# A decoder trunk on one core: x by features, packed weights, and a new order for the first weight slots

## The reference

```python
def rmsnorm(x, g):
    xf = x.astype(jnp.float32)
    y = xf * lax.rsqrt(jnp.mean(xf * xf, axis=-1, keepdims=True) + EPS)
    return (y * g.astype(jnp.float32)).astype(x.dtype)

def short_conv_mixer(h, w_in, w_conv, w_out):
    bg, cg, xv = jnp.split(h @ w_in, 3, axis=-1)
    return (bg * causal_dwconv(cg * xv, w_conv)) @ w_out

def reference(x, norm_mix, ...):
    for i in range(DEPTH):
        h = rmsnorm(x, norm_mix[i])
        if i < N_A_LAYERS:
            x = x + short_conv_mixer(h, a_w_in[i], a_conv[i], a_w_out[i])
        ...
        x = x + conv_ffn(rmsnorm(x, norm_ffn[i]), ...)
```

## Time and profile before

| | us |
|---|---|
| median of 3 runs (lowest to highest) | 579.64 (579.08 to 579.85) |
| the profiled execution, and its span | 579.68, 577.9 |
| PE busy | 570.1 (99%) |
| DVE busy | 422.0 (73%) |
| ACT busy | 318.4 (55%) |
| POOL busy | 22.5 (4%) |

### The profile page before, as it was taken

The page is one execution under the profiler, slowest core; times in us unless marked ns, Lnnn a source line. Parts: engine busy times, 40 slices in busy tenths (PEclk is TensorE's granted clock), DMA queues, the critical chain, the costliest instruction groups (busy, mean ns, idle before and its releaser), DMA issues.

```text
span 577.9 us, 8023 instructions
## 1 busy us (share of the span) xinstructions
PE 570.1 (99%) x3064; PEld 493.6 (85%) x3064; DVE 422.0 (73%) x514; ACT 318.4 (55%) x389; POOL 22.5 (4%) x26
## 2 busy tenths in 40 slices
PE   8999999999999999999999999999999999999996
PEld 7888988888888888888888899888888888888885
DVE  6898886678666666776887688896786666667764
ACT  5734463566645455456555666745656454554543
POOL 1233000000000000000000000000000000000000
PEclk9999999999999999999999999999999999999999
DMA  8996558445665565555655444285455665664001
GB/s 270 349 349 228 196 183 289 177 151 163 204 218 205 167 212 195 173 177 183 219 154 177 180 146 146 82 282 180 149 168 197 219 208 162 212 196 170 0 1 73
DMA packets 80866, 107.03 MB, mean 185 GB/s; under 512 B 1888, under 2 KB 71872, under 8 KB 80832
## 3 DMA queue, kind: packets, MB, share of 16 engines
q1 hardware_dynamic: 80240, 104.78, 55.0%
q10 hardware_dynamic: 592, 1.77, 0.9%
HBM read 105.50 MB, written 1.05 MB: 184 GB/s over the span
## 4 chain that ended last, share of the span: by engine, by line
PE 91%; DVE 2%; ACT 2%; issue 1%; SPq 1%; DMA 1%; POOL 0%; POOLq 0%; ACTq 0%
PE pair L1202 37%; PE pair L1210 19%; PE acc L1271 7%; PE acc L1275 7%; PE acc L1273 7%; PE pair L1258 5%; PE pair L1263 3%; PE acc L1178 1%; PE acc L1179 1%; PE acc L1177 1%; DVE wgt L761 1%; DMA raw<-in_a_w_in 1%; PE pair L1285 1%; ACT wgt L434 1%; ACT acc L454 0%
## 5 line engine op out<-in xcount | busy, mean ns | idle before, releaser
L761 DVE TENSOR_TENSOR wgt<-raw,wgt 128x2048 fp32r<-128x2048 f32 x92 | 211.4, 2302 | 53.6 <-ACT wgt L434 53.3
L1202 PE MATMUL pair<-hA,wgt 128*128 128x512 f32 x864 | 205.4, 391 | 0.2 <-DVE wgt L761 0.2
L434 ACT ACTIVATE wgt<-raw 128x2048 fp32r<-128x2048 f32 x93 | 177.5, 1911 | 22.9 <-PE acc L1275 21.5
L1202 PEld LDWEIGHTS pair<-hA,wgt 128*128 128x128 f32 x864 | 160.1, 188 | 32.3 <-issue 0.4
L1210 PEld LDWEIGHTS pair<-hA,wgt 128*128 128x128 f32 x864 | 107.8, 192 | 2.4
L1210 PE MATMUL pair<-hA,wgt 128*128 128x256 f32 x864 | 108.5, 283 | 0.0
L1271 PE MATMUL acc<-wgt,kq_hi 128*128 128x512 f32 x156 | 48.0, 389 | 0.0
L1275 PE MATMUL acc<-wgt,kq_lo 128*128 128x512 f32 x156 | 48.0, 389 | 0.0
L1273 PE MATMUL acc<-wgt,kq_hi 128*128 128x512 f32 x156 | 48.0, 389 | 0.0
L529 ACT ACTIVATE scratch<-scratch 128x512 f32<-128x512 f32 x22 | 13.9, 632 | 59.7 <-DVE scratch L878 59.7
L543 ACT ACTIVATE scratch<-pair 128x512 f32<-128x512 f32 x20 | 11.9, 595 | 58.3 <-PE pair L1210 58.3
(11 more groups left out here) (180 smaller groups left out, 601.9 us busy)
## 6 DMA issues: line engine op xcount, KB each, us to landing
raw<-in_ffn_w_up SPq DMA_DIRECT2D x44, 1024.0 KB, 5.1
raw<-in_ffn_w_down SPq DMA_DIRECT2D x22, 1024.0 KB, 4.9
raw<-in_a_w_in SPq DMA_DIRECT2D x10, 1024.0 KB, 11.8
raw<-in_w_kv SPq DMA_DIRECT2D x8, 1024.0 KB, 5.3
raw<-in_a_w_out SPq DMA_DIRECT2D x4, 1024.0 KB, 5.5
raw<-in_b_w_q SPq DMA_DIRECT2D x4, 1024.0 KB, 5.2
raw<-in_b_w_o SPq DMA_DIRECT2D x4, 1024.0 KB, 5.0
xs<-in_x SPq DMA_DIRECT2D x4, 256.0 KB, 4.2
```

What stands on the lines that cost most here:

```text
L434: act.activation(split_slot(s)[0], raw[:, s % RAW, :], ACT.Copy).then_inc(w_hi_ready, 2 if s + 1 in AHEAD else 1)
L761: dve.tensor_tensor(wlo, raw[:, s % RAW, :], whi.bitcast(F32), ALU.subtract).then_inc(w_lo_ready, 2 if s + 1 in AHEAD else 1)
L1202: last = pe.matmul(pair[b][:, e, :].rearrange("p (a n) -> p a n", a=2), whi[:, w], hid[:, :, k, :], start=first and k == 0, stop=not first ...
```

## The change

The host lays the inputs out anew. x comes twice: as rows (for squares and residual) and by features (`x_columns`, into `scratch`), so that PE no longer turns it. All weights lie in one array `weights`, each slot as it stands in SBUF, 8 KB per partition, in the order of use (`slot_order`); SP's loops are written out. The parameters come as one array, by features, in one transfer. The norm's gain is applied by ACT (`start_hi`, as the scale of the rounding) and by DVE (`start_lo`). The first two slots are used by turns in halves: first half of slot 0, first half of slot 1, then the second halves; slot 2 comes in halves, too. Nine fillers on a tile of ones are left. The inverse mean square is turned between the two halves of slot 2, and the convolution of the first pair is cut in two.

In the listings below a row is an engine, line and operation, what it writes and reads, and its size.

The first rows of ACT's program, with the semaphores that each row waits for. Before: a transfer of the gain, then the table load, then a square of x.

The core of the diff:

```diff
+            def x_half(g):
+
+                part = slice(g * D, (g + 1) * D)
+                sp.dma_start(scratch[:, part], x_columns[:, part]).then_inc(x_T_in[g], 16)
...
+            x_half(0)
             first_quarter(0)
...
+            load_half(1, 0, second_landed)
+            x_half(1)
+            load_half(0, 1, landed[0])
+            load_half(1, 1, landed[1])
+            x_tile(0)
+            load_half(2, 0, third_landed)
+            x_tile(1)
+            load_half(2, 1, landed[2])
+            sp.dma_start(par[:], params).then_inc(par_in, 16)
+            for s in range(3, SLOTS):
+                load(s)
...
+            def start_hi(k):
+                act.wait_ge(x_T_in[k // 4], 16)
+                act.activation(hA[:, 0, k, :], x_T0[:, k, :], ACT.Copy, scale=g_par[:, k:k + 1]).then_inc(start_hi_ready, 1)
...
+            act.dma_start(g_par[:], start_gain).then_inc(start_gain_in, 16)
+            act.wait_ge(start_gain_in, 16)
+            for k in range(3):
+                start_hi(k)
+            first_quarter_hi(1)
+            start_hi(3)
+            second_half_hi(0)
...
             mixer_cross(0, 0)
-            hi(2)
+            third_half_hi(0)
+            square(0, 1, 0)
+            square(0, 1, 1)
+            third_half_hi(1)
+            mixer_cross(0, 1)
             act.wait_ge(inv_T, 1)
             act.activation(inv_all, acc[0][0][:, 0:S], ACT.Copy).then_inc(inv_all_ready, 1)
             hi(3)
-            mixer_cross(0, 1)
             hi(4)
...
+            def start_lo(k):
+                dve.wait_ge(start_hi_ready, k + 1)
+                dve.scalar_tensor_tensor(out=hA[:, 1, k, :], in0=x_T0[:, k, :], scalar=g_par[:, k:k + 1],
+                                         in1=hA[:, 0, k, :].bitcast(F32), op0=ALU.mult,
+                                         op1=ALU.subtract).then_inc(start_lo_ready, 1)
+
+            def start_weights():
+                dve.wait_ge(first_landed[0], 16)
+                dve.tensor_copy(split_slot(0)[0][:, 0:COLS // 4], raw[:, 0, 0:COLS // 4]).then_inc(start_w_hi, 1)
...
+            dve.memset(warm_tile[:], 1.0).then_inc(warmed, 1)
+            dve.wait_ge(start_gain_in, 16)
+            start_lo(0)
+            start_weights()
+            start_lo(1)
+            start_lo(2)
+            start_lo(3)
             first_quarter_lo(1)
...
+            third_half_lo(1)
+            a_whole_sum(0, 1)
             lo(3)
-            a_whole_sum(0, 1)
-            conv_a(0)
-            lo(4)
+            c_times_x(0)
+            dve.wait_ge(par_in, 16)
+            conv_taps(0, (0,))
             for i in range(1, KD // 2):
                 a_whole_sum(i, 0)
+                if i == 1:
+                    conv_taps(0, (1,))
+                    lo(4)
                 lo(2 * i + 3)
...
+            pe.wait_ge(warmed, 1)
+            for _ in range(9):
+                pe.matmul(pair[1][:, 1, 0:P], warm_tile[:], warm_tile[:], start=True, stop=True)
...
+            for g in range(2):
+                for q in (2 * g, 2 * g + 1):
+                    first_both(q)
+                for q in (2 * g, 2 * g + 1):
+                    last = first_narrow(q)
+                if g:
+                    last.then_inc(slot_done, 1)
+                last = second_half(g)
+            last.then_inc(slot_done, 1)
+            pe.wait_ge(a_sum, a_turn(0, 0))
+            pe.wait_ge(third_hi, 1)
+            part_both(2, 0, range(KD // 2))
+            pe.wait_ge(consts, 1)
             pe.wait_ge(inv_ready, 1)
             for t in range(2):
                 last = pe.transpose(acc[0][0][:, P * t:P * t + P], inv_ms[:, t:t + 1].to_broadcast([P, P]), ident[:])
             last.then_inc(inv_T, 1)
...
+            pe.wait_ge(w_hi_ready, 3)
+            part_both(2, 0, range(KD // 2, KD))
```

More of the change, by code:

```diff
@@ L33, with slot_order, ffn, build @@
 MASKED = -1e30
-def build(nc, x, norm_mix, norm_ffn, ffn_w_up, ffn_conv, ffn_conv_b, ffn_w_down,
-          a_w_in, a_conv, a_w_out, kv_norm, w_kv, b_w_q, b_w_o, final_norm, out):
+def slot_order(D, F):
+    units = F // 256
+    order = []
+    for i in range(D // 256):
+        order += [("a_w_in", 0, D + 256 * i, False), ("a_w_in", 0, 2 * D + 256 * i, False)]
+    order += [("a_w_in", 0, 256 * i, False) for i in range(D // 256)]
+    order += [("a_w_out", 0, 256 * i, True) for i in range(D // 256)]
+    def ffn(l):
+        pieces = []
+        for j in range(units):
+            pieces += [("ffn_w_up", l, 256 * j, False), ("ffn_w_up", l, F + 256 * j, False)]
+            if j >= 2:
+                pieces.append(("ffn_w_down", l, 256 * (j - 2), True))
+        return pieces + [("ffn_w_down", l, 256 * j, True) for j in (units - 2, units - 1)]
+    order += ffn(0)
+    order += [("w_kv", None, D + 256 * i, False) for i in (0, 1, 3, 2)]
+    for i in range(D // 256):
+        order += [("w_kv", None, 256 * i, False), ("b_w_q", 0, 256 * i, False)]
+    order += [("b_w_o", 0, 256 * i, True) for i in range(D // 256)]
+    return order + ffn(1)
+def build(nc, x, x_columns, start_gain, weights, params, norm_ffn, final_norm, out, F, TAPS):
     _, S, D = x.shape
-    F = ffn_conv.shape[2]
     KD = D // P
     NH = D // P
-    TAPS = ffn_conv.shape[1]
     UNITS = F // (2 * P)
@@ L315, in ffn_loads @@
[L315 to L331, removed]
@@ L333, in x_block @@
-            def x_block(t, h):
-                sp.dma_start(xs[:, t, 512 * h:512 * h + 512], x_rows[:, t, 512 * h:512 * h + 512]).then_inc(x_in[t][h], 16)
-            def first_quarter(q):
[L339 to L343, removed]
+                sp.dma_start(raw[:, s % RAW, :], weights[s]).then_inc(landed[s % RAW], 16)
@@ L937, in conv_a, with conv_taps @@
                 dve.tensor_tensor(cx, c_all, cx, ALU.mult).then_inc(cx_ready, 1)
+            def conv_taps(i, halves=(0, 1)):
                 dve.wait_ge(cx_ready, i + 1)
-                for e in range(2):
+                for e in halves:
                     f = 2 * i + e
-                    tap = [a_par[:, (c + 1) * KD + f:(c + 1) * KD + f + 1] for c in range(TAPS)]
+                    tap = [a_par[:, c * KD + f:c * KD + f + 1] for c in range(TAPS)]
                     dve.tensor_scalar(conv_out[:, f, :], cx[:, e, :], tap[2], None, ALU.mult).then_inc(a_conv_op, 1)
```

306 lines of the change are left out of this document (118 added, 188 removed).

## The result

The changed kernel takes 583.25 us (median of 4 runs, 582.53 to 583.66) against 579.69 (median of 4, 579.08 to 579.85): ratio 1.006, interval 1.0048 to 1.0072. That is 3.56 us slower. The forecast was 580.7 with a range up to 582.4, so the time lies beyond its slow end.

A forecast was written before the change was run, and what follows sets the result against it. PE's own unbroken work was taken to bound the run after the first 30 us, so slot 4's start sets the end: 33.8 against 32.77, 1.0 later than 579.68, gave 580.7 us, range 578.4 to 582.4.

The forecast's parts named there:

- First matmul: Start: x's landing 3.8, table load 1.28, roundings and remainder put the first weight matmul at 6.5, 1.7 earlier than 8.18.
- Clock of PE: Start: the weights' matmuls begin at the lower clock level for 4.8 us (bounds 0 and 5.6), costing 2.4.
- Slot 2: Its start on PE: 6.5 + 11.11 of work + 2.4 of slow clock = 20.0, against 21.58, 1.6 gained.
- Slot 2 to slot 4: Chain through ACT and DVE takes 13.2, plus 0.6 for GpSimd; PE waits 1.8 ahead of slot 4.
- GpSimd's share: Between slots 2 and 4: GpSimd's product falls on the last three taps and holds DVE, 0.6 taken, bounds 0 and 1.29.
- slot 4 then starts at 33.8: PE's start of slot 4: 20.0 + 13.2 + 0.6 = 33.8, against 32.77, 1.0 later.
- the mark: Slot 4's start on PE, 32.77 before: the run ends as much later or sooner, unless a later wait joins in.
- At no cost: Packed weights, x loaded twice (1.05 MB more), one parameter transfer and SP's loops written out: taken as costing 0.
- (c): Rival, DVE's taps before slot 4: GpSimd shuts them out fully, 0.7 more, 581.4; chance 0.18.
- (d): Rival, start: GpSimd is shut out computing the first quarter's low half, PE stands still 1.5 us or more, 582.2; chance 0.10.
- (b): Rival, faster: the clock rises within about 1.5 us of the first matmul and taps run freely, 578.4; chance 0.24.

The follow-up runs named there:

- the usual run: The changed kernel timed once more, unaltered, against the kernel before: 583.16 us, ratio 1.0062; its profile is of a run of 583.21 us.
- the profile first taken: Profile of the changed kernel's first timing, nothing further altered: an execution of 582.53 us, the fastest of four, span 580.7, mean clock 0.999.
- the run with the held product: The changed kernel with GpSimd's second product by the inverse mean square held until DVE has the remainder of slot 4: 581.27 us, ratio 1.0028.

## Why the prediction was wrong

The sum is followed in the usual run, the last one above.

- **First matmul** (6.5): mis-sized. Measured 7.62. In the profile of the changed kernel 0.9 of the 1.1 is the landing of x (4.68 against 3.8). The table load behind it was right in place and length (1.28), and moving it away gave 1.06. With 256 KB in the first transfer x was there at 4.04, so the lower end taken from the earlier trace rows was not to be had by halving it.
- **Clock of PE** (2.4): right in kind, and near in size. From 7.62 to 20.63 is 13.01, less 11.11 of work is 1.9; in the profile first taken 2.8. That the fillers were over near 3 was wrong: each is two rows, and they ended at 5 to 5.3. It made no difference, as one filler gives the same time as nine.
- **Slot 2** (20.0): 20.63, which is 1.1 more at the first matmul and 0.5 less of slow clock. Here the change was still 0.95 ahead of the 21.58 of before.
- **Slot 2 to slot 4** (13.2 + 0.6): 34.66 - 20.63 = 14.03. The chain was right: it went by the copy, the rounding, the remainder, product, taps, sum and taps, and the wait was 2.51, inside the 1.5 to 3 that were to be seen. GpSimd's share was 0.92 (1.40 against 0.48), where 0.6 was taken between bounds of 0 and 1.29. By the Trainium skill (SBUF — State Buffer, section SBUF: two separate sides) GpSimd's product shuts a DVE operation with two SBUF inputs out for its whole length. The trace agrees: the tap that began 0.22 us behind the product ended 0.29 behind the product's end, and with the product held back it took 0.48.
- **The step that failed: slot 4 then starts at 33.8, and the run is as much later as that.** The wait was priced at its own length. In the usual run the clock falls to 0.50 just behind it, and slot 4's large matmuls lose 1.63: slot 4 is 1.89 late and the run 3.53, so the mark does not hold there. No term of the sum and none of the rivals held this. The sum with what was measured is 580.7 + 0.63 (slot 2) + 0.23 (slot 2 to 4) + 1.63 = 583.2. In the profile first taken the fall is missing, and there the mis-sized beginning makes most of the miss: 1.5 of 1.8, with slot 2 at 21.52 instead of 20.0.
- **At no cost** held for what these traces can show: no wait of PE names a load, and behind slot 4 PE waits 0.2 us in all, as before. ACT does wait for loads in the beginning, up to 1.12 us at 9.3, while PE runs at half pace. The loads came quicker, not slower: 405 GB/s from 7.6 to 21.0 and 418 from 21.0 to 33.0 in the first profile, where the kernel before had about 350 from 14 to 40. The packing of the weights was not undone by itself, so its own worth stays open.

Of the rivals, (c) was right in kind. (d) had the wrong loser: GpSimd got in at once (7.51, 1.45 us), and DVE's remainders of x were held instead, 2.30 against 1.38. The slow clock hid that; at full pace it cost PE 0.56. (b) occurred in neither profile of the changed kernel, and none of its runs came below 582.53.

What decides the verdict is shown by one move. With DVE's remainder of slot 4 ahead of the taps, and all else as changed, the time is that of before (0.9998). So nothing else in the change makes it slower on balance. With 15 fillers besides it is 0.21% faster; with the start freed of GpSimd and x in two transfers, 0.43%.

What stays open: why the fall behind a wait of 2.5 us was missing in one of the two profiles of the changed kernel. Of all six profiles with a wait of 2.5 to 2.8 ahead of slot 4, five have the fall (5.49 to 5.51 for slot 4's large matmuls) and that one has not (3.88). How long a wait must be is open as well; the one of 1.60 in the run with the held product went without a fall, in a single profile.

## What to carry to other kernels

Price a new wait of PE ahead of dense work at its length and, as a second case, with a stretch at half clock behind it; here, in the usual run, 2.5 us of wait cost 4.1. When a producer that many steps later depend on (here the remainder of the next slot) stands behind work that is needed only later (the taps), look for its due time in the consumer's queue and put it first. Fillers were worth having here only where they lasted nearly until the real work: 15 were worth 1 us, nine no more than one. In the profiles with a full pace from the first eight matmuls on, PE stood still for 0.3 to 1.1 us behind the fillers; with nine fillers it was half within these eight, behind a standstill of 1.3 as of 2.3 and more. As the runs with the shorter standstill also had more fillers, these runs do not tell which of the two counts.

## What the runs showed of the hardware

- The granted clock fell to 0.50 behind waits of PE of about 2.5 us in dense work, and the large matmuls behind lost 1.6 us, in five of six profiles. By the Trainium skill (TensorE: Matmul & The Clock Gate, section HAM oscillation — how this bites in real kernels) waits between groups of matmuls can throttle PE, and the loss is half of the throttled time. The traces agree: over 3 us at 0.50 for the 1.6 lost. The waits of the page's example are longer than those here.
- Behind nine fillers and a standstill of 2.3 us the pace fell even after the first matmuls had started: four matmuls at full pace from 7.60, then half pace from 9.33 (the run with the moved remainder alone). With 15 fillers and a standstill of 0.52, and nothing else changed, the pace stayed full.
- The profile that was read first was the fastest run of four, and its clock record (0.999) was not that of the others. Two profiles of the same kernel put the loss at different places: slot 2 stood at 21.52 and 20.63, and slot 4's large matmuls took 3.88 and 5.51.
- In the changed kernel the table load stood behind the wait ahead of ACT's first rounding (4.68 to 5.96); with a copy of 8 columns ahead of that wait it began at 1.19.
- The clock column read 1.00 in the beginning of the changed kernel's first profile, although eight matmuls took 3.79 there instead of 2.00.
